# Prompt attention and recurrence in one dense phase behind the projection, turned P copied on VectorE

## The reference

```python
h = rms_norm(x, ln_w)
proj = jnp.einsum('bsd,de->bse', h, w_in)          # 8720 columns: q, k, v of 24 heads, gates, recurrence
for g, (win, dil) in enumerate(((128, 1), (512, 4), (2048, 16))):
    o, lse = dilated_window_attn_prompt(q_g, k_g, v_g, win, dil)   # blocks of 128 rows, own and previous block
comb = softmax over g of lse, times o
step: att = where(causal, qe @ ke.T, 0); o = att @ v + qe @ state   # chunks of 64 tokens, 4 heads
      state = exp(b_last) * state + kd.T @ v
y = x + (sigmoid(ma) * (comb * silu(az)) @ w_attn_out + sigmoid(mb) * (norm(o_gla) * silu(gz)) @ w_gla_out) @ w_out
```

## Time and profile before

| | |
|---|---|
| median of 3 runs | 2471.53 us (2471.12 to 2474.16) |
| profiled execution, its own time | not listed apart; its span is 2470.5 us, 1.0 us under the median |
| busy in the span | TensorE 2439.6, VectorE 1205.1, ScalarE 906.3, GpSimd 199.2 us |
| first sample product (L1910) | 1989.4 us |
| traffic | 416.99 MB, mean 169 GB/s |

### The profile page before, as it was taken

The page is one execution under the profiler, slowest core; times in us unless marked ns, Lnnn a source line. Parts: engine busy times, 40 slices in busy tenths (PEclk is TensorE's granted clock), DMA queues, the critical chain, the costliest instruction groups (busy, mean ns, idle before and its releaser), DMA issues.

```text
span 2470.5 us, 37105 instructions
## 1 busy us (share of the span) xinstructions
PE 2439.6 (99%) x13710; PEld 1956.6 (79%) x13710; DVE 1205.1 (49%) x2860; ACT 906.3 (37%) x2163; POOL 199.2 (8%) x367
## 2 busy tenths in 40 slices
PE   9999999999999999999999999999999998999998
PEld 6888887887778888887787888788778755888887
DVE  5323432334321115565665666556756447655663
ACT  5224534443332214223544545545334233212221
POOL 0000000000000000112111111222222100000000
PEclk9999999999999999999999999999999999999999
DMA  6333323332332223457677666787677799444341
GB/s 193 103 121 115 104 92 127 104 101 92 111 107 98 91 89 122 142 170 243 210 221 227 199 210 209 220 287 226 210 227 218 221 346 349 165 153 165 141 155 69
DMA packets 209122, 416.99 MB, mean 169 GB/s; under 512 B 32512, under 2 KB 53520, under 8 KB 206832
## 3 DMA queue, kind: packets, MB, share of 16 engines
q1 hardware_dynamic: 166912, 293.60, 35.6%
q0 software_dynamic: 29712, 95.06, 13.3%
q10 hardware_dynamic: 12320, 25.96, 2.8%
HBM read 313.33 MB, written 112.99 MB: 173 GB/s over the span
## 4 chain that ended last, share of the span: by engine, by line
PE 94%; DMA 2%; DVE 2%; ACT 1%; issue 0%; SPq 0%; POOL 0%; DVEq 0%; ACTq 0%
PE b_acc L1231 20%; PE b_acc L1233 19%; PE b_acc L1232 19%; PE c_p_s L1281 3%; PE c_p_o L1304 3%; PE c_p_qk L1268 3%; PE c_p_t L1292 3%; PE f_p_b L2002 2%; PE f_p_b L2004 2%; PE f_p_b L2003 2%; PE f_p_z L2002 2%; PE f_p_z L2004 2%; PE f_p_z L2003 2%; PE b_acc L1237 1%; PE b_acc L1238 1%; PE e_p_o L1923 1%
## 5 line engine op out<-in xcount | busy, mean ns | idle before, releaser
L1231 PE MATMUL b_acc<-b_whi,hT_hi 128*128 128x512 f32 x2048 | 817.9, 399 | 4.0 <-DVE b_wlo L967 1.9
L1233 PE MATMUL b_acc<-b_whi,hT_lo 128*128 128x512 f32 x2048 | 799.3, 390 | 0.0
L1232 PE MATMUL b_acc<-b_wlo,hT_hi 128*128 128x512 f32 x2048 | 797.9, 390 | 0.0
L1231 PEld LDWEIGHTS b_acc<-b_whi,hT_hi 128*128 128x128 f32 x2048 | 384.6, 188 | 90.9 <-issue 8.7
L1233 PEld LDWEIGHTS b_acc<-b_whi,hT_lo 128*128 128x128 f32 x2048 | 384.5, 188 | 82.7
L1232 PEld LDWEIGHTS b_acc<-b_wlo,hT_hi 128*128 128x128 f32 x2048 | 385.3, 188 | 74.2
L967 DVE SCALAR_TENSOR_TENSOR b_wlo<-b_raw,a_lnw,b_whi 128x512 fp32r<-128x512 f32 x268 | 192.7, 748 | 364.6 <-ACT b_whi L759 364.2
L773 ACT COPY b_stage<-b_acc 128x512 f32<-128x512 f32 (+2 forms) x198 | 115.3, 582 | 506.6 <-PE b_acc L1233 496.1
L797 ACT ACTIVATE c_sm<-c_sm,c_ends 128x256 f32<-128x256 f32 (+1 forms) x384 | 172.9, 452 | 81.6 <-DVE c_ends L1052 81.6
L759 ACT ACTIVATE b_whi<-b_raw,a_lnw 128x512 fp32r<-128x512 f32 x268 | 182.9, 714 | 4.1 <-ACT c_og L815 1.9
L771 ACT ACTIVATE b_stage<-b_acc 128x512 f32<-128x512 f32 x96 | 57.4, 598 | 306.4 <-PE b_acc L1233 306.2
(11 more groups left out here) (320 smaller groups left out, 3153.4 us busy)
## 6 DMA issues: line engine op xcount, KB each, us to landing
b_raw<-in_w_in SPq DMA_DIRECT2D x134, 512.0 KB, 4.2
tm<-b_stage SPq DMA_DIRECT2D x256, 256.0 KB, 2.1
a_x<-tm POOLq DMA_DIRECT2D x192, 256.0 KB, 4.8
b_ck<-in_cache_kv_w POOLq DMA_DIRECT2D x104, 256.0 KB, 5.0
c_qk<-tm SPq DMA_DIRECT2D x101, 256.0 KB, 3.6
f_m<-tm SPq DMA_DIRECT2D x16, 1024.0 KB, 5.8
c_v<-tm SPq DMA_DIRECT2D x53, 256.0 KB, 4.2
og<-c_og ACTq DMA_DIRECT2D x48, 264.0 KB, 3.8
```

Source lines behind the costliest of these rows:

```text
L1231: nc.tensor.matmul(out, stat_hi, mov_hi, start=(k == 0), stop=False)
L1232: nc.tensor.matmul(out, stat_hi, mov_lo, start=False, stop=False)
L1233: return nc.tensor.matmul(out, stat_lo, mov_hi, start=False, stop=(k == KC - 1))
```

## The change

`plan_attention` now starts behind the last slot: 48 tasks in the order group 2 (16 near), group 1, group 0, each task four steps long, a pair at every even step from 588 on. The tasks without queries are gone. `plan_recurrence` starts seven steps later and runs once through all 16 tiles, eight steps apart, woven into the attention pairs; the last tile starts at step 762, the last pair at 778, and the phase ends at step 786. In `attend(q)` each engine does its attention steps first, then `recur(q)`, then the sample tail.

- All copies of turned P are VectorE's. Exponentials and masks have four buffers `sm` in place of two.
- Attention's buffers (`plan_phase`) lie where projection weights lay, so first uses wait until the last weights, products and stores are done.
- The recurrence has PSUM banks of its own (the projection's `b_acc`), its state three buffers, and its k is turned into `c_p_qk` as a fourth kind of `transposes`. The state no longer goes to DRAM in between; constants are loaded and buffers cleared once.
- The squares of the recurrence output are made by POOL (product) and VectorE (sum) in place of ScalarE.
- In the late stage eight V pieces (3 to 10) go to the freed input buffers, pieces 11 and 12 and the loads of `lse` stand behind `attention_over`, on which TensorE's, VectorE's, POOL's and SP's late main now wait too.

```diff
+def plan_attention(first):
+    tasks = [Task(2, r, 0, False) for r in range(16)]
+    tasks += [Task(1, r, a, a > 0) for r in range(4) for a in range(4)]
+    tasks += [Task(0, 0, a, a > 0) for a in range(NT)]
+    units = [Unit(4 * i + c, i, c, first + 4 * i + 2 * (c // 2)) for i in range(len(tasks)) for c in range(4)]
...
-            tile_at[GBLK * k + j] = at + (11 if k % 2 == 0 else 10) + 6 * j
+            tile_at[GBLK * k + j] = at + 11 + 8 * j
+        at = tile_at[GBLK * k + GBLK - 1] + 9
...
+    FIRST_Q = 2 * NSLOT
+    tasks, units = plan_attention(FIRST_Q)
+    g_at, t_at = plan_recurrence(FIRST_Q + 7)
...
+    for i in range(N_TASK):
+        turn_qk_at[units[4 * i].q - 4] = (i, 1)
+        turn_qk_at[units[4 * i].q - 2] = (i, 0)
+        turn_qk_at[units[4 * i].q + 9] = (i, 2)
+    for n, at in t_at.items():
+        turn_qk_at[at + 1] = (n, 3)
...
+        def attention_over(eng):
+            eng.wait_ge(pv_done, N_U)
+            eng.wait_ge(o_turned, N_TASK)
+            for k in range(2):
+                eng.wait_ge(og_out[k], 16 * N_TASK // 2)
...
+                    if i == 0:
+                        sp.wait_ge(mm_done, NSLOT)
...
+                for n in range(NT):
+                    pool.wait_ge(go_evacd, n + 1)
+                    y = gout[:, n % 2, :].rearrange("p (h e) -> p h e", h=GH)
+                    if n >= 1:
+                        pool.wait_ge(squared, n)
+                    nc.gpsimd.tensor_tensor(gjunk[:, :, :], y, y, ALU.mult).then_inc(go_mult, 1)
...
-                def pT_evac(x):
-                    b = slice(1, 4, 2) if is_near(x) else slice(0, 4)
-                    act.wait_ge(pt_done, x.u + 1)
...
+                    for x in turn_p_at.get(q, ()):
+                        pT_evac(x)
...
+                def squares(n):
+                    dve.wait_ge(go_mult, n + 1)
+                    V.tensor_reduce(gss[:, GH * n:GH * n + GH], gjunk[:, :, :], AX_X, ALU.add).then_inc(squared, 1)
...
                 def attend(q):
-                    recur(q)
-                    late_tail(q - LATE)
                     for x in score_at.get(q, ()):
                         scores(x)
...
+                    recur(q)
+                    late_tail(q - LATE)
...
-HV_TILES, HV_PAIRS, HV_ROWS = range(5, 9), range(9, 13), range(18, 25)
+HV_TILES, HV_PAIRS, HV_ROWS = range(3, 7), range(7, 11), range(18, 25)
...
+            over.attention_over(sp)
+            load_v(11)
+            load_v(12)
+            load_lse()
```

More of the change, by code:

```diff
@@ L152 @@
 G_STEPS = 15
-Task = namedtuple("Task", "g res block prev queries half")
+Task = namedtuple("Task", "g res block prev")
 Unit = namedtuple("Unit", "u i c q")
[L157 to L189, removed]
+def plan_attention(first):
[3 more added lines that the diff above has]
+    units = [Unit(4 * i + c, i, c, first + 4 * i + 2 * (c // 2)) for i in range(len(tasks)) for c in range(4)]
@@ L289, in project @@
[L289 to L297, removed]
@@ L298, in project @@
-    tqk_free = {what: (at + 1) // 2 for at, what in turn_qk_at.items()}
-    g_at, t_at = plan_recurrence((80, begin + 97))
+    last_unit = lambda i: units[4 * i + 3]
+    g_at, t_at = plan_recurrence(FIRST_Q + 7)
     gates_of, tile_of = {q: k for k, q in g_at.items()}, {q: n for n, q in t_at.items()}
     LATE = t_at[NT - 1] + 7
-    last_of = [max(x.u for x in units if tasks[x.i].half == half) for half in range(2)]
-    tasks_by = [len([i for i in u0 if tasks[i].half <= half]) for half in range(2)]
+    LAST_Q = max(units[-1].q + 8, LATE + 11)
@@ new lines, in project @@
+    turn_qk_at = {}
+    for i in range(N_TASK):
[4 more added lines that the diff above has]
+        turn_qk_at[at + 1] = (n, 3)
+    assert len(turn_qk_at) == 3 * N_TASK + NT
+    tqk_no = {turn_qk_at[at]: n + 1 for n, at in enumerate(sorted(turn_qk_at))}
+    turned_first = {what: [sum(1 for i, a in tqk_no if a == kind and tqk_no[i, a] < n) for kind in range(4)]
+                    for what, n in tqk_no.items()}
@@ L308, in stored_by @@
+    tqk_free = {what: (at + 1) // 2 for at, what in turn_qk_at.items()}
     def stored_by(chunk, half):
@@ L628, in _ @@
                         load_pair(p)
-                for s in range(NSLOT + 1):
+                for s in range(SP_END):
                     if s - 2 in gated_no:
                         store(s - 2)
-                    if s >= 1 and s - 1 not in gated_no:
+                    if 1 <= s <= NSLOT and s - 1 not in gated_no:
                         store(s - 1)
@@ L1467 @@
 Late = namedtuple("Late", "sync gpsimd tensor scalar vector")
[L1468 removed]
+Projection = namedtuple("Projection", "mm_done stored scored products stores scores new_scores recurrence_over weights_over attention_over")
 def plan_late(nc):
@@ L1780, in tail, with load_lse @@
                     sp.dma_start(dst, src).then_inc(tables_in, 16)
-            if q in (1, 2, 3):
-                load_v(q + 1)
+                for k in range(STAGES):
+                    sp.wait_ge(over.stored[k], over.stores[k])
+                load_v(2)
+        def load_lse():
+            for t in range(0, NT, 4):
+                for g in range(3):
+                    sp.dma_start(lse[:, t:t + 4, g, :], OG[:, g, CH:].rearrange("(t p) c -> p t c", p=P)[:, t:t + 4, :]
+                                 ).then_inc(tables_in, 16)
         def tile(t):
@@ L1813, in main @@
                 load_v(w)
-            for k in range(STAGES):
-                sp.wait_ge(over.stored[k], over.stores[k])
             for i in range(6):
@@ L2069, in main @@
         def main():
+            over.attention_over(pe)
             pv_new(0)
```

466 lines of the change are left out of this document (200 added, 266 removed).

## The result

The changed kernel takes **2604.8 us** (median of 4 runs, 2600.6 to 2606.2) where the kernel before takes 2472.9 beside it: ratio 1.0532, 95% interval 1.0517 to 1.0547. Slower, as forecast, but by 132 us and not 44, and outside the range of 2484 to 2545. The profiled execution spans 2604.4 us, against 2470.5.

What follows compares the result with a forecast made beforehand. TensorE's own work and rare waits were taken to bound the kernel: 2470.5 us, plus phase 430 (attention 318, recurrence 84, gates 28), plus edges 15, less moved work 401.7, plus 1.0 outside the span, gave 2515 us (2484 to 2545).

Steps and rivals of the forecast that it cites:

- The price of the moved work: In the projection before the change: attention and recurrence woven between its matmuls cost 401.7 us (320.7 attention, 81.0 recurrence).
- Projection slots at 0.2252 us a matmul throughout, ending near 1588 us: Sign to look for in the projection: without woven work it runs at this rate until the phase starts.
- Gates, 28 us: Four gates in the phase: 4.5 us of TensorE, plus 6 of ScalarE's 7.9 us shown on TensorE each time.
- Recurrence, 11 x 2.1 us: In the phase: TensorE stands 2.1 us for VectorE's scaling at each of 11 tiles that fall on far tasks.
- the ring: Chain of turns, copies and exponentials over two pairs, closed by one bank for turns: about 6.0 us a near task.
- TensorE's work, 7.16 a task, covers it: In far tasks (two blocks): TensorE's own 7.16 us hides the chain of turns, copies and exponentials.
- Near tasks, 6.0 us: Tasks on their own block only: 6.0 us each in the first group, where TensorE has 4.5 us of work.
- Granted clock 1.00: Sign to look for in the phase: TensorE keeps its full granted clock.
- My clock rival: Near tasks run at 1.2 GHz: 48 us more, 2563 us; chance 0.15, shared with starved loads.
- Edges, 15 us: Around the phase: 6 us at its start, 4 near its end, 5 behind it for the last attention store.
- Sample stage, 0 with -12 to +15: After the phase: moved V pieces and queued loads of maxima and sums change this stage by 0 us.
- Copies of P, 0: In the phase: the 96 copies moved from ScalarE to VectorE cost nothing; without cover 96 x 0.6 us at most.

Runs made afterwards that it cites:

- combo4: The changed kernel with the edits of q_scale and lse_own, and window copies issued three at a time behind each recurrence tile's squares on POOL's queue: 2515.3 us.
- q_scale: The changed kernel with Q copied ahead of the exponentials on ScalarE and a tile's scaling at the head of its step on VectorE: 2537.9 us.
- lse_own: The changed kernel with the twelve row-sum loads on their own semaphore, so the first sample turns wait for their three tables alone: 2587.2 us.

## Why the prediction was right and wrong

The step that failed is the cost of what TensorE waits for once the cover is gone. The phase with its edges was to take 445 us and took 499.4: the gates (28 us) and the rings of the tasks were sized by adding up passes, without the order in which each queue makes them. Two more terms stood at nothing: the transfers that stay in the projection (11.8 us measured) and the sample stage (24.4).

- **The direction and its reason** held: the moved work cost the projection 401.7 us, and no order tried brought phase and edges under 431 with all its work, or under 424 without ScalarE's gate passes. The Trainium skill's rule on regimes (Perfetto Trace Analysis, Optimization Strategy) pointed the same way, and every run here agrees with it.
- **The price of the moved work** held: with the window copies out of the way the first scores came at 1588.7 us, against 1587.7.
- **"Projection slots at 0.2252 us a matmul throughout, ending near 1588 us"** failed. I costed the transfers of the phase, not those that stay: in a projection 400 us shorter, broadcasts, caches and window copies fall into less time. 11.8 us, of which combo4 gave back 10.8 by the place of the window copies (q_scale without it starts its scores at 1599.9).
- **Gates, 28 us,** was the largest single failure. I took 6 of ScalarE's 7.9 us a gate and 1 of TensorE; a gate cost some 10 to 20 us (the estimate above), about 30 of the 54 that the phase is over. I had summed passes without asking which copy stands behind them: output copy, four exponentials and the Q copy, in that order. q_scale shows the order to be a part of it (29 us less in the pairs behind the gates), but in the good order a gate still costs about 11, of which ScalarE's passes are 2 to 2.5. What the rest would fall to without VectorE's passes wasn't tried.
- **Recurrence, 11 x 2.1 us,** had the wait at the right place but not its twin. Nine tiles fall on far tasks, not eleven, and nine waits of 2.0 us were measured (18.4 us). At the seven on near tasks the same turn waits 1.7 us for the bank that Q holds, where I let the ring hide it. The 3.8 us a tile for TensorE is near the truth (36.5 - 4 x 7.16 is 3.9 a tile), though seven switches of 0.1 us in 16 tiles leave 70 us and not the 65 that I wrote.
- **"TensorE's work, 7.16 a task, covers it"** is about right for eight far pairs at 41.4 us against 40.4, and right once the order is mended: 36.5 against 36.2 without the 2.1s. At 0.24 us a task it is some 6 us of the 54.
- **Near tasks, 6.0 us:** (34.2 - 7.6) / 4 = 6.65. Too low by a tenth, some 15 us over 21 near tasks; in the good order (28.7 - 7.6) / 4 = 5.3, under my ring. The ring wasn't a property of the work but of the order of one queue.
- **Granted clock 1.00** failed: 0.92 over the phase. My clock rival named the wrong place, the near tasks with their many small idles (0.95 in 1643 to 1676 us). The lowest readings came behind single stands, of 5.2 to 6.3 us at the gates but also of 2.7 and 3.0, which I had not forecast because I had spread each gate's cost as a sum.
- **Edges, 15 us,** were about right in sum (TensorE's waits there are 15.3 us) and not in their parts. At the start K and Q are turned inside the last slots, but TensorE stands 3.0 us for a later load of K (4.5 in combo4), so a wait on loads, one of my signs of being wrong, is there too. Near the end it stands 4.2 us at 2066.7, where VectorE prepares the sample probabilities (L2312 to L2317, 2059.1 to 2063.3 us) ahead of its masks; I had named a load. The store of the last output is 3.3 (such a store lands in 2.1 in the median, where the earlier trace rows had 3.8).
- **Sample stage, 0 with -12 to +15:** +24.4. I saw the twelve loads "queue at its head" and left them at 0. They cost 14 us through a semaphore shared with a turn that doesn't need them; in combo4 11 us remain, where it waits 6.8 for a V cache (1.7 before).
- **Copies of P, 0:** right in the kernel before (0.1%), and -5.6 or +22.9 us for their undoing, by the order around them.
- **Squares, 0,** and the recurrence's own banks, "already in these sums", were not tested: no run undoes them.
- That combo4 lands on my 2515 is chance: its phase is 13 us under the forecast and its sample stage 11 over.

Open: what is left in combo4, 42 us over the kernel before, is 30 us of phase over what the moved work cost in the projection, 11 of sample stage and 1 of projection. What a second bank for the turns would give, which would part Q, K, output and keys, wasn't tried: scores, turned P, the output, the turns and the recurrence take all eight.

## What to carry to other kernels

When work loses its cover, write down for every engine what stands behind each long pass in program order, and who waits for that: here the place of one 0.6 us copy and three 0.4 us scalings was worth 67 us, more than any size that I had argued about. Two waits in one ring hide each other: try the fixes together before you call one of them worthless. And when a stage gets shorter, cost what stays in it too: transfers that were spread over it, and semaphores that count loads of different urgency.

## What I had not expected of the hardware

- Adding 21 us of products of no use to TensorE made the kernel 9.1 us faster, by filling stands of 5 to 6 us ahead of small matmuls. Filling stands of 2 to 3 us changed nothing in time, though the clock had fallen behind one of them too (16 scores in 2.08 us behind 2.9).
- A wait that the profile gave to "issue" (TensorE's turn of the output) ended 0.1 us behind VectorE's K copy at the three gates read above: it was a wait for that engine.
- The same 4400 TensorE instructions showed 404 us busy at a granted 0.92 and 381 at 0.97: a change in "busy" can be the clock alone.
- A table load of ScalarE takes 1.28 us with the next pass right behind it (1830.95, then 1832.25). The Trainium skill (ScalarE: Activation LUTs, What ACT_TABLE_LOAD costs) gives about 1.38 us more for a drain; no row here shows it.
- Of twelve loads of small rows that SP issued one behind the other, ten took 0.5 to 1.1 us each, and the fourth and fifth 5.6 and 4.9 us, here and in lse_own and combo4 alike (6.5 and 5.2, 5.6 and 5.1). Why these two is not shown.
